# Moving a filter's transforms from the attention to the pauses at two norms, and writing the MLPs' first quarter without clearing

## The reference, cut to what matters

```python
for i in range(2):
    u_l = modulate(rms_norm_2(h_lat, norm_mix_pre[i]), ...)
    y_l = differential_attention(u_l, u_c, ...)   # i == 0, 8 heads, softmax over 768 keys, two maps a head
    y_l = hyena_mixer(u_l, ...)                   # i == 1
    h_lat = h_lat + mod_l[2] * rms_norm_2(y_l, norm_mix_post[i])
    v_l = modulate(rms_norm_2(h_lat, norm_mlp_pre[i]), ...)
    h_lat = h_lat + mod_l[5] * rms_norm_2(squared_relu_mlp(v_l, w_mlp_in[i], w_mlp_out[i]), norm_mlp_post[i])

def hyena_filters(...):        # depends on weights alone, not on x
    ...
    h = (hdn @ w_out).reshape(n, 2, D_MODEL)
    h = h * jnp.exp(-t * deltas[None, :])[:, None, :]
    return h[:, 0], h[:, 1]    # h_fwd, h_bwd

def two_sided_fft_conv(v, h_fwd, h_bwd):
    kern = jnp.concatenate([h_fwd, jnp.zeros((1, ...)), h_bwd[:0:-1]], axis=0)
    vf, kf = jnp.fft.rfft(v, n=2 * n, axis=1), jnp.fft.rfft(kern, n=2 * n, axis=0)
    return jnp.fft.irfft(vf * kf[None], n=2 * n, axis=1)[:, :n]
```

## Time and profile before

| | |
|---|---|
| time, median of 3 runs | 3503.87 us (3500.01 to 3505.92) |
| the profiled execution | 3500.37 us, span 3498.6 us |
| TensorE busy | 3240.3 us, 93% of the span, 16146 matmuls |
| DVE busy | 1819.7 us, 52% |
| ScalarE busy | 1077.6 us, 31% |
| GpSimd busy | 1267.6 us, 36% |
| granted TensorE clock, mean | 0.96 |

### The profile page before, as it was taken

One profiled execution on the slowest core, in us unless ns is written; L12 is line 12 of the kernel. 1 busy time (PEld: TensorE's weight loads), 2 busy tenths in 40 slices (PEclk: granted clock), 3 DMA queues, 4 the chain that ended last, 5 costly groups with the idle time before them and its releaser, 6 DMA issues.

```text
span 3498.6 us, 38584 instructions
## 1 busy us (share of the span) xinstructions
PE 3240.3 (93%) x16146; PEld 2656.2 (76%) x16146; DVE 1819.7 (52%) x2233; ACT 1077.6 (31%) x1415; POOL 1267.6 (36%) x394
## 2 busy tenths in 40 slices
PE   5999998989898999989999899888999989789998
PEld 4988878777877788779887677646888767568886
DVE  4663575757584443545446566554222465852224
ACT  2222243333332332222223344333222332142221
POOL 2334343333333343333433311113444443444443
PEclk8999999999999999999999899889999999889998
DMA  4454421111121233335444111101333333023331
GB/s 135 147 173 138 137 102 61 61 61 62 59 73 49 84 97 97 97 123 178 145 157 129 49 37 37 49 36 61 96 97 97 96 108 109 0 71 98 97 97 60
DMA packets 278703, 319.99 MB, mean 91 GB/s; under 512 B 6771, under 2 KB 244994, under 8 KB 278339
## 3 DMA queue, kind: packets, MB, share of 16 engines
q1 hardware_dynamic: 239808, 245.38, 22.1%
q10 hardware_dynamic: 38722, 72.15, 5.9%
HBM read 311.22 MB, written 6.29 MB: 91 GB/s over the span
## 4 chain that ended last, share of the span: by engine, by line
PE 77%; DVE 15%; issue 3%; ACT 3%; DMA 1%; POOL 1%; ACTq 0%; DVEq 0%; SPq 0%; POOLq 0%; another core or an unknown queue 0%
PE ps L471 21%; PE ps L473 21%; PE ps L472 21%; DVE rs L1830 3%; PE psx L879 2%; PE psx L677 1%; PE ps L704 1%; PE ps L911 1%; PE psx L471 1%; PE psx L472 1%; PE psx L473 1%; DVE KB L1835 1%; DVE QB L1835 1%; PE psx L638 1%; DVE PB L1849 1%
## 5 line engine op out<-in xcount | busy, mean ns | idle before, releaser
L308 POOL TENSOR_TENSOR Wl<-Wr,Wh 128x2048 fp32r<-128x2048 f32 x232 | 1069.9, 4614 | 1816.1 <-ACT Wh L1108 1816.0
L471 PE MATMUL ps<-Ah,Wh 128*128 128x512 f32 x2016 | 812.0, 403 | 42.0 <-DVE Al L1650 29.6
L473 PE MATMUL ps<-Ah,Wl 128*128 128x512 f32 x2016 | 790.6, 392 | 0.0
L472 PE MATMUL ps<-Al,Wh 128*128 128x512 f32 x2016 | 790.4, 392 | 0.0
L1108 ACT ACTIVATE Wh<-Wr 128x2048 fp32r<-128x2048 f32 x232 | 443.0, 1909 | 361.8 <-DMA Wr<-in_w_mlp_in_dram 109.1
L471 PEld LDWEIGHTS ps<-Ah,Wh 128*128 128x128 f32 x2016 | 382.1, 190 | 134.7 <-issue 53.5
L472 PEld LDWEIGHTS ps<-Al,Wh 128*128 128x128 f32 x2016 | 382.2, 190 | 86.8 <-issue 9.4
L473 PEld LDWEIGHTS ps<-Ah,Wl 128*128 128x128 f32 x2016 | 381.4, 189 | 81.6
L471 PE MATMUL ps<-Yh,Wh 128*128 128x512 f32 x1088 | 426.2, 392 | 4.4 <-DVE Yl L1701 2.6
L472 PE MATMUL ps<-Yl,Wh 128*128 128x512 f32 x1088 | 424.6, 390 | 0.0
L473 PE MATMUL ps<-Yh,Wl 128*128 128x512 f32 x1088 | 424.6, 390 | 0.0
(11 more groups left out here) (350 smaller groups left out, 4049.1 us busy)
## 6 DMA issues: line engine op xcount, KB each, us to landing
Wr<-in_a_w_in_dram SPq DMA_DIRECT2D x48, 1024.0 KB, 8.0
modw<-in_w_mod_dram ACTq DMA_DIRECT2D x96, 512.0 KB, 5.8
Wr<-in_b_w_in_dram SPq DMA_DIRECT2D x40, 1024.0 KB, 5.1
Wr<-in_w_mlp_in_dram SPq DMA_DIRECT2D x32, 1024.0 KB, 5.7
Wr<-in_w_mlp_out_dram SPq DMA_DIRECT2D x32, 1024.0 KB, 5.2
Wr<-in_a_w_out_dram SPq DMA_DIRECT2D x16, 1024.0 KB, 5.4
Wr<-in_c_w_in_dram SPq DMA_DIRECT2D x16, 1024.0 KB, 5.7
Wr<-in_attn_w_qkv_dram SPq DMA_DIRECT2D x12, 1024.0 KB, 5.1
```

The lines of the kernel that those rows point to most:

```text
L308: pool.tensor_tensor(E.Wl[:, s, :], E.Wr[:, s, :], E.Wh[:, s, :].bitcast(F32), ALU.subtract).then_inc(*LO.did(p))
L471: pe.matmul(o, ah, bh, start=first, stop=False)
L472: pe.matmul(o, ah, bl, start=False, stop=False)
L473: return pe.matmul(o, al, bh, start=False, stop=last)
```

## The change

Three things change.

The k units leave the attention. `FILTER_AT` now holds one w unit for each of the steps 25 to 32, and nothing behind. The loads of `woF` and `dlF` stand in step 23 instead of 24, and wait for the end of the attention's last weight tile, since these buffers now lie in `Ah`; the table `tabF` is loaded in step 32. The k units of the first half of the channels are done in D's post and M0's norm, those of the second half in M0's post and H's norm: `beside` on TensorE (two matmuls into one bank, eight calls in each pause), `halves` on ScalarE (two copies for each k unit, into `fY`, which lies over `Yh` and `Yl`), `folded` on GpSimd (sum and difference), and `keep` on ScalarE (four stores to `kspec`). In M0 ScalarE and DVE wait for the stores before they write the third tile of `Yh` and `Yl`.

In H the norm stands ahead of the gate and of the loads; the load of the first half's spectrum moves to the fourth panel, behind the wait for the stores.

The memsets of `yt` go; the first quarter of an MLP writes its results with `tensor_scalar` instead of adding them.

```diff
-FILTER_AT = {25: (("w", 0, 0), ("w", 0, 1)), 26: (("w", 0, 2), ("w", 0, 3)), 27: (("w", 1, 0), ("w", 1, 1)), 28: (("w", 1, 2), ("w", 1, 3)),
-             29: (("k", 0, 0, 0),), 30: (("k", 0, 0, 1),), 31: (("k", 0, 1, 0),), 32: (("k", 0, 1, 1),),
-             33: (("k", 1, 0, 0), ("k", 1, 0, 1)), 34: (("k", 1, 1, 0), ("k", 1, 1, 1))}
+FILTER_AT = {25 + 4 * half + t: (half, t) for half in range(2) for t in range(TT)}
+BESIDE = [(fi, w) for fi in range(2) for w in range(2)]
...
 def pool_program(E, pool):
...
-    def post(L, zero):
+    def post(L, half=None):
         pool.wait_ge(*A.of("post_in", L))
-        for k in range(KD):
-            if k % 2:
-                pool.wait_ge(*V.of("pt", L, k))
-                pool.tensor_tensor(x[:, k, :], x[:, k, :], tmp[:, k % 4, :], ALU.add).then_inc(*G.did("px", L, k))
-            if zero:
-                pool.wait_ge(*V.of("pt", L, k))
-                pool.memset(E.yt[:, k, :], 0.0).then_inc(*G.did("yz", L, k))
+        for k in range(1, KD, 2):
+            pool.wait_ge(*V.of("pt", L, k))
+            pool.tensor_tensor(x[:, k, :], x[:, k, :], tmp[:, k % 4, :], ALU.add).then_inc(*G.did("px", L, k))
+        if half is not None:
+            folded(half, 0)
+            folded(half, 1)
+
+    def folded(half, n):
+
+        fi, w = BESIDE[n]
+        o = spectrum(E, n)
+        even, odd = o[:, 1, :], o[:, 2, :]
+        pool.wait_ge(*A.of("F", "odd", half, fi, w))
+        pool.tensor_tensor(o[:, 0, :], even, odd, ALU.add).then_inc(*G.did("F", "sum", half, fi, w))
+        pool.wait_ge(*G.of("F", "sum", half, fi, w))
+        pool.tensor_tensor(even, odd if w else even, even if w else odd, ALU.subtract).then_inc(*G.did("F", "kc", half, fi, w))
...
     def hyena():
         norm("H", E.Ah, E.Al)
+        folded(1, 2)
+        folded(1, 3)
...
 def pe_program(E, pe):
...
+    def beside(half, n, e):
+
+        if half is None:
+            return
+        fi, w = BESIDE[n]
+        b = ((4, 5), (2, 3), (4, 5), (6, 7))[n][e]
+        if n + e == 0:
+            pe.wait_ge(*G.of("F", "hs", half, TT - 1))
+            if half == 0:
+                pe.wait_ge(*E.signals["ld_t"].of(1))
+        into(b)
+        for k in (2 * e, 2 * e + 1):
+            m = pe.matmul(bank[b], E.tabF[:, w, k, fi * P:(fi + 1) * P], E.hsF[:, half, w, k, :], start=(k == 2 * e), stop=(k == 2 * e + 1))
+        m.then_inc(*X.did("F", "k", half, fi, w, e))
+        emptied[b] = A.of("F", "odd" if e else "even", half, fi, w)
+
+    def post(L, last, half=None):
+        beside(half, 0, 0)
         into(7)
         pe.wait_ge(*V.of("acc", L))
         rms_sum(E.acc, psx[:, 3, :], ("rsum2", L))
...
+        beside(half, 0, 1)
+        beside(half, 1, 0)
         into(6)
         for k in range(KD):
             pe.wait_ge(*A.of("psq", L, k))
             square_sum(k, ("pss", L, k) if k < KD - 1 else ("summed", L + "+"))
+            if k == 2:
+                beside(half, 1, 1)
...
 def act_program(E, act):
...
+    def halves(half, n):
+
+        fi, w = BESIDE[n]
+        for e, o in ((0, "even"), (1, "odd")):
+            b = ((4, 5), (2, 3), (4, 5), (6, 7))[n][e]
+            act.wait_ge(*X.of("F", "k", half, fi, w, e))
...
+            act.activation(spectrum(E, n)[:, 1 + e, :], psx[:, b - 4, :] if b >= 4 else ps[b][:], ACT.Copy).then_inc(*A.did("F", o, half, fi, w))
+
+    def keep(half):
+        for n, (fi, w) in enumerate(BESIDE):
+            act.wait_ge(*G.of("F", "kc", half, fi, w))
+            act.dma_start(E.kspec[w].rearrange("(r f) p n -> f p r n", r=2)[fi, :, :, half * 512:half * 512 + 512],
+                          spectrum(E, n)[:, 0:2, :]).then_inc(*STK[half].did(fi, w))
...
+                    if L == "M0" and iq == 0 and c == 2:
+                        act.wait_ge(*STK[0].of(*BESIDE[-1]))
                     act.activation(Yh[:, c, :], tmp[:, b, :], ACT.Copy).then_inc(*A.did(L, "yh", iq, c))
+                if L == "M0" and iq + n == 0:
+                    keep(0)
                 ahead(L, "i", iq, n)
...
     def hyena():
         LDH = E.signals["ld_h"]
+        norm("H", E.Ah, "M0", lambda k: shift(E, 1, 0, k), "M0+", half=1)
         gate("M0")
-        act.wait_ge(*STK[0].of(1, 1))
-        act.wait_ge(*STK[1].of(1, 1))
...
-        norm("H", E.Ah, "M0", lambda k: shift(E, 1, 0, k), "M0+")
...
 def dve_program(E, dve):
...
-            out_y(L, iq, add=(lambda c: V.of(L, "o", iq - 1, c)) if iq else (lambda c: G.of("yz", zeroed, c)), squares=iq == 3)
+            if iq == 0:
+                dve.wait_ge(*V.of("pt", before, KD - 1))
+            out_y(L, iq, add=(lambda c: V.of(L, "o", iq - 1, c)) if iq else None, squares=iq == 3)
```

More of the change, by code:

```diff
@@ L979, in attention, with mlp @@
                 T.also("h_end", "D")
-            step(n, FILTER_AT.get(n, ()))
+            step(n, FILTER_AT.get(n))
         out("D", 0)
-        post("D", False)
-    def mlp(L, last):
+        post("D", False, 0)
+    def mlp(L, last, half=None):
+        if L == "M0":
+            for n in (2, 3):
+                for e in range(2):
+                    beside(0, n, e)
         for iq in range(4):
@@ L998, in mlp @@
             out(L, iq)
-        post(L, last)
+        post(L, last, half)
     def hyena():
+        for n in (2, 3):
+            for e in range(2):
+                beside(1, n, e)
         nb = 0
@@ L1134, in norm @@
             act.wait_ge(*T.of("h_end", free))
+        if half is not None:
+            halves(half, 2)
         for k in range(KD):
@@ L2089, in attention @@
                 tile(n // 8 + 1, n % 8)
-            for what in f[1:]:
-                filt(*what)
             if n < D_UNITS:
```

220 lines of the change are left out of this document (96 added, 124 removed).

## The result

The change takes 3460.45 us (median of four runs, 3457.72 to 3462.16) against 3504.55 us before (median of four, 3500.01 to 3505.92). The ratio is 0.9882, with a 95% interval from 0.987 to 0.9895: 1.2% faster. The forecast was 3464 for the median. The profiled execution took 3457.72 us with a span of 3455.7 us; the forecast for it was 3460.7.

The account below looks back on a forecast made before the run. TensorE holds 77% of the last chain, but time is to be had only where it waits or works on something else. 37.7 + 4.2 - 2.2 = 39.7 off 3500.37 gives 3460.7, median 3464; range 3448 to 3479.

Parts of the forecast that it names:

- Part 1: Attention steps 25 to 31: one filter unit a step and earlier loads take six steps from 82.4 to 63.4, gain 19.0.
- The full-clock sum: Attention steps 25 to 31: six steps take 52.8 us if TensorE keeps its full clock.
- Part 2: Attention's tail to the output projection: 37.2 us becomes 16.5, gain 20.7 (19 to 23); projection's half-clock start loses 2.
- Part 3: Transforms in the two pauses: cost 0 at full clock, GpSimd's additions lie in its idle time, small gain from full-clock starts.
- The bound of 10: Transforms in the pauses: if TensorE is at half clock there, up to 10 us lost for both pauses.
- Part 4: Hyena's norm goes ahead of its gate: the square root can start at 2808.8, 3.15 us gained.
- Part 5: Stores in the first MLP: folds and issues delay the third panel's high part, a stall of 2.2 us (0 to 5).
- Part 6: No clearing of yt: sixteen memsets of 0.5 us go, gain taken as 0 (bound 1).
- the first rival: Clock stays up in all new steps and the tail: steps 52.8, tail 14.5, total 3452 or below; 15%.
- Half clock all through: Half clock in steps, tail and pauses: steps 74, tail 18.4, total 3488, or 3478 without the pauses; 17%.
- late loads: The filter's loads in the attention still come late: the 6.38 wait stays, steps begin cold, total 3470; 8%.
- the slower case: TensorE stays at half clock through the output projection, 38 us extra, and as long again in the MLP's first panels; 2%.

Follow-up runs that it names:

- the second run: The change with two w units in each of steps 25 to 28, the second's matmuls behind the values, its DVE products behind the weights; 3466.0 us.
- the second profile: The change itself, unaltered, run again on the chip of the other runs: 3457.15 us, ratio 0.9877 to the kernel before.
- the last run: The change with two w units in each of steps 25 to 28, the second behind values (TensorE) and weights (DVE); 3466.0 us, single run.

## Why the forecast was right, and where not

It named the right stages and the right sign, and the total came out 3.5 us below the forecast for the median and 3.0 below that for the profiled time. That closeness is partly luck: parts 1 and 2 gave 9 us more than forecast, and against that the MLP gave 3.4 less and the two pauses 2.9 less; another 0.6 came from stretches that the forecast left alone.

**Part 1, the steps.** The mechanism held in this: no wait for dlF, one unit a step. The full-clock sum was 52.8 us and 52.7 were measured; part of that agreement is luck, too. A plain step took 7.8 us and not 8.05, a square root with its table loads cost 1.65 and not 1.28, and the first step lost 0.5 to half clock. The step that failed is "At half clock, 1.2 GHz, that is 12.3 us and is the bound", and with it the choice of the middle, 63.4. The clock did swing (0.65 in one step, 0.59 in step 24), but in the whole step at 0.65 TensorE was busy for 9.38 us and the step took what it took at full clock. I had priced six steps that are at half clock from end to end, and none of the six was. Where such a step did run cold for most of its length, as step 28 at 0.59 in the run with the memsets, it lost 0.45 us. What "the clock was 0.64" in the earlier trace rows meant is answered by the two runs with pairs: a step with two units takes some 13 us, and step 27 of the second run took 12.6 even at full clock. The term was mis-sized by 10.7 us; against that step 24, which I took as unchanged, lost 0.95 (7.29 us instead of 6.34) to half clock, and 1.7 in the second profile. The loads ahead of it are not its cause: in the run with two units they stand at the same place, and its step 24 takes 6.35. The forecast weighed two sections of the Trainium skill, TensorE: Matmul & The Clock Gate. The second ("A second HAM failure mode: psum-queue depth-cycling") describes what the rows show, a clock that swings (0.65 in step 27, 1.00 in the steps on either side) with holes of 0.28 to 1.44 us between groups of matmuls. The time came out as by the first all the same, since the swing stayed under cover.

My account of the 13.7 us a step of before was half right. The pair is the largest part of it, 13.7 us over the six steps by the run with two units. But "the second stands on DVE behind the maxima" is not enough: moving it behind the values on TensorE and behind the weights on DVE gave back only 3.8 of them. That DVE's four products and their slowing beside GpSimd hold most of the rest is likely from the rows of the last run, and not shown.

**Part 2, the tail.** Forecast 16.5 (14.5 to 18.4), measured 17.6; the projection's cold start was put at 2 us and cost 2.7, and 2.1 in the second profile. The upper end, "18.4 with TensorE's parts doubled", was too low: at a clock of 0.57 the same tail took 21.5. Within it "the values now 11.2 us, with one k unit of 3.5 in it: some 8.2" forgot that the eighth w unit takes the k unit's place (and 11.2 less 3.5 is 7.7): 12.4 us were measured, with 2.5 for that unit and flips and values partly at half clock. The way from there to the projection took 5.15 where I had 6.3.

**Part 3, the transforms.** Held for TensorE: its matmuls cost nothing in either pause, by the run without them. The bound of 10 was far off, because TensorE's transforms ran at full clock in both pauses. GpSimd's folds, which "lie in its idle time", did cost: they are the loss of part 4 and a part of that of part 5.

**Part 4, the hyena's norm.** This failed, and the cause is a reading error. The step that failed is "Now it can start at 2808.8: 3.15 us gained". The text ahead of the prediction says that the norm stands ahead of the gate, and its excerpt of the diff shows the two lines in that order. In the change the gate comes first, on ScalarE and on DVE, and the norm behind it; only the six loads and the wait for the stores went behind the norm. The gate waits for the end of GpSimd's part of the MLP, and to that the change has added two folds. So the root was freed of 3.15 us of issues and held for 3.2 us by the folds, and came 22.6 us behind the last square of the MLP where it came 22.4 before. The 0.9 us for a warmer start came: seven cold matmuls instead of fourteen, the first tile 19.3 us behind the root instead of 20.4, 0.9 us in the pause as a whole. The run with the order that I had described then gave the 3.35 us.

**Part 5, the stores.** Right place, wrong size: 2.2 forecast with 5 as the bound, 5.6 lost. The step that failed is "Folds and issues move it 2.5 us": the high part came 8.7 us behind the first tile's copy (2405.43 to 2414.15) where it came 3.9 before, 4.8 later. Three things were short. Four stores take 3.12 us of issue, not four times 0.5. I had folds and squares of DVE side by side without a price, and each square took more than twice its time. And behind a stop of 3.74 us TensorE ran at half clock (0.69 in the row of 2420.71), 1.6 us more. The Trainium skill has the middle one: SBUF — State Buffer, section "Who interferes with whom", says that DVE and GpSimd share a pair of ports that one of them holds at a time. The trace agrees: a square takes 0.69 us alone, 1.47 and 1.78 beside the folds and 4.62 beside the split of a panel, and each of the three ends 0.55 us behind the end of GpSimd's operation (2406.99, 2410.39 and 2420.65).

```profile
2416.58 4.62 DVE L2141 TENSOR_TENSOR tmp<-tmp 128x512 f32<-128x512 f32 x1 [4.25 <-ACT tmp L1563]
```

**Part 6, the memsets.** Held: nothing.

The rivals: the steps took the time of the first rival, full clock, though the clock did not stay up; its 14.5 for the tail and the gain ahead of the hyena did not come, which kept the time from its 3452. Half clock all through, late loads and the slower case did not come.

## What to carry to other kernels

Before pricing a stretch at half clock, ask what else bounds it: step 27 lost a third of its clock and nobody waited, while a step without filler (6.35 us) lost up to 1.7 and the tail, a chain through TensorE, 4.0. A unit of filler work belongs once in a step, and behind the work that the chain needs on every engine that it touches: a step without a unit took 6.35 us, with one 7.8, with two 13.9 and with the second one behind the chain 12.6. When work is added to an engine near a stage's end, look for the gates that wait for that end: a wait on "all of the stage before" takes in the new work unasked.

## What the runs showed of the hardware

Additions of GpSimd, 1.3 to 1.6 us each, more than doubled the time of DVE's squares beside them, which ended 0.55 us behind them each time. The 1.7 us that this cost by itself became 3.3 with the stores: the stop grew by 1.8, and the matmuls behind it ran at half clock for 1.6 more.

The tail of the attention took 17.5 to 17.6 us in six profiles and 21.5 in two, with the same code in it; the granted clock was 0.73 to 0.77 in the one kind and 0.57 or 0.58 in the other.

The issue of four stores of 128x2x512 took 3.12 us on ScalarE's queue at 2410.98, with the high part behind it. Three such stores in the hyena took 1.56 while ScalarE worked on a high part of 1.91 us. The first had to wait for nothing but the issue itself; why an issue takes 0.78 us here and 0.5 there stays open.

One program's stretch of some 260 us in the hyena differed by 1.4 us between two profiles. For differences of 3 us, events in the traces decide, not medians.
